# Moving the root multiplication of three modulation loops to GpSimd, and the unrounded value to VectorE, in a two-layer diffusion trunk

## What is computed

```python
def rmsnorm(x, g):
    y = xf * lax.rsqrt(jnp.mean(xf * xf, axis=-1, keepdims=True) + NORM_EPS)
    return (y * g).astype(x.dtype)

def modulate(h, shift, scale):
    return h * (1 + scale) + shift

        x = x + g1 * rmsnorm(y, norm_g[l, 1])
        h = modulate(rmsnorm(x, norm_g[l, 2]), sh2, sc2)
        x = x + g2 * rmsnorm(ffn(h), norm_g[l, 3])
```

## Time and profile before

| | before |
|---|---|
| median of 3 runs | 2117.55 us (2115.91 to 2119.34) |
| profiled execution | 2113.5 us, span 2111.7 us |
| mean granted TensorE clock | 0.959 |
| PE busy | 1962.5 us, 93% of the span |
| VectorE (DVE) busy | 1321.0 us, 63% |
| ScalarE (ACT) busy | 1115.2 us, 53% |
| GpSimd (POOL) busy | 28.2 us, 1%, 44 instructions |
| affine halves of the three loops, L406 | 48 of 586 ns (median) |
| rounding copies, L411 | 24 of 631 ns |
| low parts, L392 | 24 of 692 ns |

### The profile page before, as it was taken

The page is one execution under the profiler, slowest core; times in us unless marked ns, Lnnn a source line. Parts: engine busy times, 40 slices in busy tenths (PEclk is TensorE's granted clock), DMA queues, the critical chain, the costliest instruction groups (busy, mean ns, idle before and its releaser), DMA issues.

```text
span 2111.7 us, 25390 instructions
## 1 busy us (share of the span) xinstructions
PE 1962.5 (93%) x9566; PEld 1540.6 (73%) x9566; DVE 1321.0 (63%) x1259; ACT 1115.2 (53%) x1130; POOL 28.2 (1%) x44
## 2 busy tenths in 40 slices
PE   5998798999999989788799999999999999999996
PEld 2786474888878659347688788787878878788785
DVE  2344736222323261464688888888888888888885
ACT  3433535222222352344477777776777677677773
POOL 0000000000000000130000000000000000000000
PEclk9999999999999989799699999999999999999998
DMA  9443153622222154221499898998989989899990
GB/s 320 131 160 120 36 184 102 196 91 91 100 82 98 60 182 132 73 67 41 142 345 366 306 367 310 357 368 304 365 311 367 366 304 365 310 368 341 334 364 39
DMA packets 263893, 473.27 MB, mean 224 GB/s; under 512 B 17112, under 2 KB 116368, under 8 KB 263824
## 3 DMA queue, kind: packets, MB, share of 16 engines
q1 hardware_dynamic: 262928, 469.31, 63.2%
q0 software_dynamic: 896, 3.02, 0.5%
HBM read 471.25 MB, written 1.05 MB: 224 GB/s over the span
## 4 chain that ended last, share of the span: by engine, by line
PE 81%; DVE 9%; ACT 5%; issue 4%; DMA 2%; DVEq 0%; SPq 0%; ACTq 0%
PE bank L478 23%; PE bank L480 23%; PE bank L479 23%; PE bank L345 2%; DMA raw_weights<-in_w_mod 2%; PE bank L632 2%; PE bank L1635 2%; DVE split_low L1399 2%; PE bank L525 2%; ACT overlay L406 1%; PE bank L1677 1%; PE bank L607 1%; DVE y L1386 1%; PE bank L622 1%; DVE overlay L419 1%
## 5 line engine op out<-in xcount | busy, mean ns | idle before, releaser
L1399 DVE TENSOR_TENSOR split_low<-raw_weights,split_high 128x2048 fp32r<-128x2048 f32 x224 | 511.7, 2287 | 59.5 <-ACT split_high L1099 58.6
L1099 ACT ACTIVATE split_high<-raw_weights 128x2048 fp32r<-128x2048 f32 x224 | 429.0, 1919 | 147.3 <-PE bank L480 147.2
L462 DVE TENSOR_TENSOR split_low<-raw_weights,split_high 128x1024 fp32r<-128x1024 f32 x118 | 143.8, 1225 | 341.2 <-ACT split_high L457 341.1
L478 PE MATMUL bank<-h_high,split_high 128*128 128x512 f32 (+1 forms) x848 | 329.1, 388 | 28.8 <-DVE h_low L392 18.5
L479 PE MATMUL bank<-h_low,split_high 128*128 128x512 f32 (+1 forms) x848 | 323.7, 382 | 0.0
L480 PE MATMUL bank<-h_high,split_low 128*128 128x512 f32 (+1 forms) x848 | 323.4, 381 | 0.0
L1399 DVE TENSOR_TENSOR h_low<-raw_weights,h_high 128x2048 fp32r<-128x2048 f32 x112 | 256.7, 2292 | 77.8 <-ACT h_high L1099 77.8
L478 PE MATMUL bank<-split_high,xe_high 128*128 128x512 f32 x672 | 271.7, 404 | 14.2 <-DVE split_low L1399 14.2
L480 PE MATMUL bank<-split_high,xe_low 128*128 128x512 f32 x672 | 266.2, 396 | 0.0
L479 PE MATMUL bank<-split_low,xe_high 128*128 128x512 f32 x672 | 266.1, 396 | 0.0
L1099 ACT ACTIVATE h_high<-raw_weights 128x2048 fp32r<-128x2048 f32 x112 | 214.8, 1918 | 43.0 <-PE bank L480 43.0
(11 more groups left out here) (237 smaller groups left out, 2710.0 us busy)
## 6 DMA issues: line engine op xcount, KB each, us to landing
raw_weights<-in_moe_w SPq DMA_DIRECT2D x336, 1024.0 KB, 7.0
raw_weights<-in_w_mod SPq DMA_DIRECT2D x48, 1024.0 KB, 7.4
raw_weights<-in_ffn_w SPq DMA_DIRECT2D x33, 1024.0 KB, 5.3
raw_weights<-in_ev_w_in SPq DMA_DIRECT2D x10, 1024.0 KB, 11.7
raw_weights<-in_od_w_in SPq DMA_DIRECT2D x8, 1024.0 KB, 9.1
raw_weights<-in_ev_w_out SPq DMA_DIRECT2D x4, 1024.0 KB, 11.1
raw_weights<-in_od_w_out SPq DMA_DIRECT2D x4, 1024.0 KB, 6.9
overlay<-in_rpb SPq DMA_DIRECT2D x32, 64.0 KB, 2.3
```

The costliest lines, as they stand in the source:

```text
L462: dve.tensor_tensor(half_of(s, j, SPL[:, s % NSPLIT, :]), half_of(s, j, raw_of(split_at[s])), half_of(s, j, SPH[:, s % NSPLIT, :]).bitcast ...
L478: pe.matmul(ps, wh, xh, start=first, stop=False)
L1099: act.activation(esplit(u)[0], RAW[:, u % NRAW, :], ACT.Copy).then_inc(S("e_high"), 1)
L1399: dve.tensor_tensor(lo, RAW[:, u % NRAW, :], hi.bitcast(F32), ALU.subtract)\
```

## The change

In n0, n2 and n4 the multiplication by RS moves from VectorE to GpSimd (`pool_modulate`). Its tile t waits, from the third on, until both readers of the TMP buffer are done (`_hh` and `_hf` at t-1). ScalarE makes scale * TMP + shift in two halves and writes HH itself, in the fp32r type; its copy is gone. VectorE makes the same scale * TMP + shift for itself, unrounded, in two halves into HF, waits for that and for HH, and subtracts. The multiplications are no longer two tiles ahead by their place in a list; GpSimd runs ahead as far as the two buffers allow. `first` in n0 stands ahead of the loop, behind a wait for the vectors. The reciprocal counts on a semaphore of its own ("rstd"), for which GpSimd waits too. n6 keeps its work under other names.

```diff
         def dve_rstd(dve, n):
             dve.wait_ge(*norm_root(n["name"]))
             r = n["rs"][:, :n["width"]]
-            link(dve, dve.reciprocal(r, r))
+            dve.reciprocal(r, r).then_inc(S("rstd"), 1)
+            dve.wait_ge(S("rstd"), n["index"] + 1)
...
+        def pool_modulate(pool, n):
+            wd = n["width"]
+            pool.wait_ge(S("rstd"), n["index"] + 1)
+            for t in range(n["nt"]):
+                if t >= 2:
+                    pool.wait_ge(S(n["name"] + "_hh"), t - 1)
+                    pool.wait_ge(S(n["name"] + "_hf"), t - 1)
+                pool.tensor_tensor(TMP[:, t % 2, :wd], n["src"](t), RS[:, :wd], ALU.mult)\
+                    .then_inc(S(n["name"] + "_tmp"), 1)
...
+        def dve_modulate(dve, n, l, which, c0, first=None):
+            a, sh = mod_vectors(l, which)
             nt, wd = n["nt"], n["width"]
+            dve.wait_ge(S("affine"), 1 + 2 * l + which)
+            if first:
+                first(0, 0)
+            for t in range(nt):
+                dve.wait_ge(S(n["name"] + "_tmp"), t + 1)
+                for v, a0, a1 in halves(c0):
+                    last = dve.tensor_scalar(HF[:, t % 2, a0:a1], TMP[:, t % 2, a0:a1], a[:, t, v:v + 1],
+                                             sh[:, t, v:v + 1], ALU.mult, ALU.add)
+                last.then_inc(S(n["name"] + "_hf"), 1)
+                dve.wait_ge(S(n["name"] + "_hf"), t + 1)
+                dve.wait_ge(S(n["name"] + "_hh"), t + 1)
+                dve.tensor_tensor(HL[:, t, c0:TOK], HF[:, t % 2, :wd], HH[:, t, c0:TOK].bitcast(F32),
+                                  ALU.subtract).then_inc(S(n["name"] + "_hl"), 1)
+
+        def act_modulate(act, n, l, which, c0):
+            a, sh = mod_vectors(l, which)
+            for t in range(n["nt"]):
+                act.wait_ge(S(n["name"] + "_tmp"), t + 1)
+                for v, a0, a1 in halves(c0):
+                    last = act.activation(HH[:, t, c0 + a0:c0 + a1], TMP[:, t % 2, a0:a1], ACT.Identity,
+                                          bias=sh[:, t, v:v + 1], scale=a[:, t, v:v + 1])
+                last.then_inc(S(n["name"] + "_hh"), 1)
...
             pool.dma_start(SBB, bass.AP(w["sgu_b"].tensor, 0, [[0, P], [1, 512]])).then_inc(S("sgu_b_in"), 16)
+            for name in ("n0", "n2", "n4"):
+                pool_modulate(pool, N[name])
```

More of the change, by code:

```diff
@@ L368, in dve_rstd @@
             r = n["rs"][:, :n["width"]]
-            link(dve, dve.reciprocal(r, r))
+            dve.reciprocal(r, r).then_inc(S("rstd"), 1)
+            dve.wait_ge(S("rstd"), n["index"] + 1)
         def mod_vectors(l, which):
             return VEC[:, l, 2 * which], MOD[:, l, 24 * which:24 * which + 8]
-        def dve_modulate(dve, n, c0, full=False, first=None):
-            nt, wd = n["nt"], n["width"]
-            def tmp(t):
+        def pool_modulate(pool, n):
[7 more added lines that the diff above has]
+                    .then_inc(S(n["name"] + "_tmp"), 1)
@@ new lines, in act_modulate, with dve_scale @@
+        def act_modulate(act, n, l, which, c0):
[6 more added lines that the diff above has]
+                last.then_inc(S(n["name"] + "_hh"), 1)
+        def dve_scale(dve, n):
+            wd = n["width"]
+            for t in range(n["nt"]):
@@ L383, in tmp, with act_shift @@
                    .then_inc(S(n["name"] + "_tmp"), 1)
[L385 to L397, removed]
+        def act_shift(act, n, l, which):
             a, sh = mod_vectors(l, which)
-            nt, wd = n["nt"], n["width"]
-            for t in range(nt):
+            for t in range(n["nt"]):
                 act.wait_ge(S(n["name"] + "_tmp"), t + 1)
[L402 to L411, removed]
+                act.activation(HFULL[:, t, :], TMP[:, t % 2, :n["width"]], ACT.Identity, bias=sh[:, t, 1:2],
+                               scale=a[:, t, 1:2]).then_inc(S(n["name"] + "_h"), 1)
         def dve_residual(dve, n, l, which, c0):
@@ L1054, in _ @@
             act_root(act, N["n6"])
-            act_modulate(act, N["n6"], 1, 1, 256, full=True)
+            act_shift(act, N["n6"], 1, 1)
             act_table(act, ACT.Exp, 51)
@@ L1163, in _ @@
             dve_affine(dve, 0, 0, 1.0, 8).then_inc(S("affine"), 1)
-            dve_modulate(dve, N["n0"], 0, first=to)
+            dve_modulate(dve, N["n0"], 0, 0, 0, first=to)
             for g, s in run("ev"):
@@ L1219, in _ @@
             dve_rstd(dve, N["n2"])
-            dve_modulate(dve, N["n2"], 0)
+            dve_modulate(dve, N["n2"], 0, 1, 0)
             dve_mods(dve, 6, 8, 7)
@@ L1247, in _ @@
             dve_rstd(dve, N["n4"])
-            dve_modulate(dve, N["n4"], 0)
+            dve_modulate(dve, N["n4"], 1, 0, 0)
             for g, s in run("od"):
@@ L1269, in _ @@
             dve_rstd(dve, N["n6"])
-            dve_modulate(dve, N["n6"], 256, full=True)
+            dve_scale(dve, N["n6"])
             dve_mods(dve, 11, 12, 7)
```

## The result

| | before | changed |
|---|---|---|
| median of 5 runs | 2116.9 us | 2130.93 us (2126.49 to 2132.29) |
| profiled execution | 2113.5 us, span 2111.7 | 2131.25 us, span 2129.4 |
| loop n0, reciprocal's end to the last low part | 15.2 us | 20.4 us |
| loop n2 | 14.97 us | 19.15 us |
| loop n4 | 14.96 us | 19.12 us |

The ratio is 1.006, with a 95% interval from 1.0046 to 1.0074: the kernel is slower by 14 us in the medians. The three loops account for 5.2 + 4.18 + 4.16 = 13.5 us of it.

What follows compares the result with a forecast made beforehand. ScalarE's pair and copy, 1.65 us a tile, were taken to bound the three loops. Collisions with GpSimd (+14.0 us) and a slower clock (+4.2) made +18.2 on the 2117.55 us median: 2135.8 us, range 2121 to 2144.

Steps and rivals of the forecast that it cites:

- The path: Loops n0, n2, n4: ScalarE's pair and copy set 1.65 us a tile; loop gains or losses carry to the end.
- The collision: Loops n0, n2, n4: VectorE's pair and subtraction exclude GpSimd's multiplication, cycle 2.36 us against 1.65, together 14.0 us.
- The step taken from two rows of another stage: Attention masks: SBUF-to-SBUF tensor_scalar ended 0.29 us after GpSimd, so the loops' affine operation would stand still too.
- the choice to treat the subtraction like it: Loops: VectorE's subtraction, two SBUF inputs, taken as held beside GpSimd like L710; both held given 0.60.
- The hop from VectorE to GpSimd: Loops: delay before GpSimd starts after VectorE, taken as 0.29 us, bounds 0.03 and 0.29.
- GpSimd's start: Loop n0: first GpSimd arithmetic, 6.5 us after its pool setup, costed at 0, other end 6.5 us.
- The clock: Behind n0 and n2: TensorE leaves the loop at granted clock 0.50, losing 2.1 us twice, +4.2 (bounds 0 and 4.2).
- The 0.51 us wait for the split: After n0: TensorE's wait for the second weight half disappears, taking 0.51 us off that loop's loss.
- The step at fault: Behind n0 and n2: clock expected to stay 0.50 for 4.5 us of work as behind n4, 2.1 us lost each.
- n4's 4.5 us: Behind n4 in the kernel before: unbroken TensorE work at granted clock 0.50, ten 512-column products done instead of 19.
- The sum: Whole kernel: 14.0 us in the loops plus 4.2 of clock, +18.2 us, giving 2135.8 us.

Runs made afterwards that it cites:

- e6: Kernel before, with VectorE instead of ScalarE making the rounding copy of every second tile, GpSimd not used: ratio 0.9988 (0.9975 to 1.0001).
- e9: Kernel before, with VectorE making the odd tiles' rounding copy and multiplying tile t+2 ahead of tile t's subtraction: ratio 0.9977 (0.9968 to 0.9986).
- e2: Changed kernel with the multiplication by the root back on VectorE, GpSimd idle in the loops: ratio to the kernel before 1.0009 (0.9999 to 1.0019).
- e5: Kernel before with only the multiplication moved to GpSimd; ScalarE keeps pair and rounding copy: ratio 1.002 (1.0007 to 1.0033).
- e1: Changed kernel with VectorE's unrounded value written to and subtracted from PSUM banks: ratio to the kernel before 1.0009 (0.9998 to 1.002).
- e3: Changed kernel with the subtraction replaced by a product with one PSUM input, pair still in SBUF, low parts left out: 1.89 us a tile.
- e4: Changed kernel with the pair writing PSUM and the subtraction replaced by a product of two SBUF inputs, low parts left out: 1.69 us a tile.
- e8: Changed kernel, unaltered, measured again beside the others: ratio to the kernel before 1.0055 (1.0033 to 1.0077), median 2129.58 us.

## Why the prediction was right

**The path, right.** ScalarE's pair and copy set the old 1.65 us; e6 and e9 show it, since taking part of the copy off ScalarE alone shortens the loops. That the loops' time passes on one for one holds within 1 to 2 us: 13.5 us in the loops and 14 in the medians (9.7 to 15.7), in e9 -4.5 and -5.5 (-3.0 to -6.8). It is not shown more closely: e2 has 4.6 in the loops and 2.7 in the medians (at most 4.0), e5 2.0 and 4.1.

**The collision, right.** The step taken from two rows of another stage (L710 ending 0.29 us behind GpSimd) and from the choice to treat the subtraction like it gave a cycle of 2.36; 2.33 was measured. Its parts: GpSimd alone 1.26 (1.29 predicted), 1.13 to 1.15 behind VectorE (1.14), the pair behind GpSimd 0.47 (0.48), the first low part 3.76 us after the reciprocal (3.94), the last 19.15 (19.50), n0 20.4 (20.7). In n0 the turns came in another order than predicted: the vectors, which the prediction had at nothing, take 1.06 us behind the first multiplication, the split stands behind the second, and the first pair is then not held (0.72). The turns add up to nearly the same time in either order, so n0's number is right in part by that. The hop from VectorE to GpSimd was 0.08 at the loop's start and 0.14 behind the pair, not 0.29; the row that I took it from was a DMA issue. It hardly counted, as it lay under the subtraction. e1, e3 and e4 show both halves. The Trainium skill's sentence on the shared port pair (SBUF — State Buffer, SBUF: two separate sides) agrees with them: operations with two SBUF inputs and the SBUF-to-SBUF pair are held, and neither is with one operand in PSUM.

**GpSimd's start, right.** Its first multiplication took no longer than the others; nothing was paid for the setup of the earlier trace rows, which here lies 6.4 us ahead of it.

**The clock, mis-sized.** This term of the sum (+4.2) failed. The clock was at 0.50 at the ends of n0 and n2, as predicted, but in n2 it was not for 4.5 us behind the loop. Behind n2 in the changed kernel:

```profile
378.80:381.10 2.30, 2.30 (x6) 1.82 (x6) 2.27 (x4) 0.59 (x2) 0.00 (x0) 0.50 0.03 7
381.10:393.80 12.70, 12.70 (x57) 10.52 (x56) 4.24 (x5) 3.56 (x5) 0.00 (x0) 1.00 0.95 297
```

The 15 us behind n0 and n2 in the changed kernel:

```profile
69.90:84.90 15.00, 15.00 (x58) 12.18 (x58) 5.83 (x5) 6.90 (x9) 0.00 (x0) 0.86 0.57 182
378.80:393.80 15.00, 15.00 (x62) 12.34 (x62) 6.50 (x8) 4.15 (x5) 0.00 (x0) 0.92 0.81 253
```

against the same stretches of the kernel before:

```profile
65.50:80.50 15.00, 14.49 (x63) 11.68 (x63) 6.67 (x6) 7.99 (x10) 0.00 (x0) 1.00 0.65 210
365.30:380.30 15.00, 14.97 (x66) 12.40 (x67) 6.89 (x8) 4.71 (x6) 0.00 (x0) 1.00 0.81 255
```

Behind n2, 62 products in place of 66, at 0.235 us 0.9 us; behind n0, 58 in place of 63, 1.2 us. In e8 it is 63 and 62, 0.7 and 0.2 us. The 0.51 us wait for the split is gone, as predicted, and is in these counts. I had put down 2.1 us twice, less the 0.5: 3.7 against 0.9 to 2.1 measured. The step at fault took n4's 4.5 us as the price after any slow loop; in n2 the products sped up 2.3 us after the last low part (at 381.1, and after 2.3 us in e8 too), in n0 4.1 us after it (at 73.9) and in e8 2.7 us after it. Why the same loop end is followed by 4.1 us in one run and 2.7 in another stays open.

**The sum.** 18.2 us predicted; loops 13.5 and the clock 0.9 to 2.1 make 14.4 to 15.6; the medians show 14.0 and the interval 9.7 to 15.7. The 18.2 itself lies above this interval; the range was wide enough since its lower end had the clock at nothing. The profiled execution's span grew by 17.7 us, more than that. From the end of loop n0 to the end of n2's reciprocal it took 289.7 us where the profile of before has 284.9; e8 has 288.4, e5 286.9 and e6 285.0. One part of it, from the first head's reciprocal to n1's, took 75.4 us in the profile of before and 77.0 to 77.2 in all others, e6 without GpSimd among them, so 1.6 us belong to a favourable profile of before and not to the change. Of the remaining 3.3 us (1.9 in e8) the clock behind n0 is a part. But e9, with shorter loops than the kernel before and no work for GpSimd in them, took 288.4 us there, e1 288.1 and e2 287.7. So most of what the profile shows beyond the loops comes without a slow n0 too, and cannot be put down to the change; what moves this stretch from profile to profile stays open.

## What to carry to other kernels

Before work goes to GpSimd, look at the operands of what VectorE does at the same time: with two input tensors in SBUF, or an fp32 tensor_scalar from SBUF to SBUF, the two engines took turns here, and their times add up (here 1.27 + 0.48 + 0.74, less a start-up). A loop whose cycle is set by one engine may cover this; as soon as VectorE is the bound, it is a straight loss. Look first for the idle time of VectorE itself: sharing out a copy, with the next tile's work ahead of the waiting operation, gave 5 us, where the change lost 14.

## What I had not expected

- A VectorE operation of 16 columns took 1.06 us in place of 0.17, because it has two inputs in SBUF and started 0.23 us after a GpSimd operation. In proportion the small operation was hit hardest.
- A tensor_scalar of 256 columns costs 0.54 us with a PSUM bank as its output, against 0.41 to SBUF; that ate the whole gain of freeing GpSimd (e1).
- The subtraction was never held in the changed kernel, 691 to 693 ns, but up to 1759 in e5: whoever comes first has the other wait, and in the changed kernel VectorE's own semaphore (0.03 us) beat the hop to GpSimd (0.14) every time.
- Two more products a tile left the granted clock at 0.50 from 780 us to the end of n4 (792.9), while it was 1.00 at n0's end. What separates the two stays open.
